# Scoring the cached keys of a decoder step: the products of queries and keys move from GpSimd to VectorE

## The reference, cut to what matters

```
tmat = lax.linalg.triangular_solve(lower + eye, eye, left_side=True, lower=True, unit_diagonal=True)
u = tmat @ (vc * bc[..., None])
w = tmat @ (kb * jnp.exp(gcum)[..., None])
def step(S, xs):
    v_new = u_i - einsum('bhck,bhkv->bhcv', w_i, S)
    o_i = einsum(q_i * exp(g_i), S) + einsum(qk_i, v_new)
    S = S * exp(g_last) + einsum(k_i * exp(g_last - g_i), v_new)
```

```
past_k = cache_k[l][page_table].reshape(Bd, past_len, H_FOX, HEAD_DIM)
s = jnp.einsum('bqhd,bkhd->bhqk', qi, k_all).astype(jnp.float32) * scale
```

## Time and profile before

| | us |
|---|---|
| median of 3 runs | 1795.97 |
| lowest and highest | 1795.91, 1796.79 |
| time of the profiled execution | 1795.97 |
| its span, first to last instruction | 1794.3 |
| what lies around the span | 1.7 |
| the stage `delta_rule`, from 455.6 to 643.3 of the span | 187.7 |
| mean granted TensorE clock of the span | 0.92 |

### The profile page before, as it was taken

How to read it: one execution, slowest core, us unless ns; L and a number is a source line. 1 busy time by engine, 2 the same in 40 slices (tenths; PEclk the granted TensorE clock), 3 DMA queues, 4 the chain that set the end, 5 groups by cost and what they waited for, 6 DMA issues and landing times. The chain is left out here.

```text
span 1794.3 us, 32705 instructions
## 1 busy us (share of the span) xinstructions
PE 1645.4 (92%) x13778; PEld 1513.6 (84%) x13778; DVE 801.2 (45%) x1362; ACT 404.4 (23%) x696; POOL 236.4 (13%) x272
## 2 busy tenths in 40 slices
PE   5999999666899979788799899999999999999995
PEld 5899999564689867465588799999999999999995
DVE  5227862473377622355556333423424424424426
ACT  4210000331222210154555321111111111111112
POOL 3000000240788600011000100000000000000003
PEclk9999999755799975699899899999999999999998
DMA  6011110200223231132243021111110110120122
GB/s 187 24 47 47 47 47 23 90 3 1 72 74 87 61 92 18 53 89 72 101 146 106 26 71 36 48 59 36 48 59 27 55 61 24 49 71 24 47 94 96
DMA packets 113657, 108.52 MB, mean 60 GB/s; under 512 B 16294, under 2 KB 103807, under 8 KB 113509
## 3 DMA queue, kind: packets, MB, share of 16 engines
q1 hardware_dynamic: 110453, 105.56, 19.0%
q0 software_dynamic: 3072, 1.07, 0.5%
HBM read 93.98 MB, written 12.93 MB: 60 GB/s over the span
## 5 line engine op out<-in xcount | busy, mean ns | idle before, releaser
L2354 DVE TENSOR_TENSOR ff_acc<-ff_acc,mf_ps 128x344 f32<-128x344 f32 x264 | 135.3, 513 | 187.4 <-PE mf_ps L2497 187.3
L2490 PE MATMUL mf_ps<-h_lo,ff_w_hi 128*128 128x344 f32 x1008 | 213.8, 320 | 0.0
L2490 PE MATMUL mf_ps<-h_hi,ff_w_hi 128*128 128x344 f32 x1008 | 213.6, 320 | 0.0
L2490 PE MATMUL mf_ps<-h_hi,ff_w_lo 128*128 128x344 f32 x1008 | 212.7, 319 | 0.0
L2497 PE MATMUL mf_ps<-ff_h_hi,ff_d_hi 128*128 128x344 f32 x528 | 170.3, 322 | 3.7 <-DVE ff_h_lo L2349 3.7
L2497 PE MATMUL mf_ps<-ff_h_hi,ff_d_lo 128*128 128x344 f32 x528 | 169.9, 322 | 0.0
L2490 PEld LDWEIGHTS mf_ps<-h_hi,ff_w_lo 128*128 128x128 f32 x1008 | 169.2, 188 | 0.0
L2497 PE MATMUL mf_ps<-ff_h_lo,ff_d_hi 128*128 128x344 f32 x528 | 169.2, 321 | 0.0
L2490 PEld LDWEIGHTS mf_ps<-h_hi,ff_w_hi 128*128 128x128 f32 x1008 | 169.1, 188 | 0.0
L2490 PEld LDWEIGHTS mf_ps<-h_lo,ff_w_hi 128*128 128x128 f32 x1008 | 168.8, 188 | 0.0
L2225 POOL TENSOR_TENSOR ff_x<-ff_x,ff_scaled 128x1024 f32<-128x1024 f32 x7 | 16.4, 2359 | 765.3 <-DVE ff_scaled L2361 765.3
(11 more groups left out here) (424 smaller groups left out, 2637.4 us busy)
## 6 DMA issues: line engine op xcount, KB each, us to landing
fs_keys<-in_cache_k_dram SPq DMA_DIRECT2D x64, 192.0 KB, 2.6
fs_values<-in_cache_v_dram SPq DMA_DIRECT2D x64, 192.0 KB, 2.5
in_raw<-in_w_in_dram SPq DMA_DIRECT2D x22, 512.0 KB, 3.9
ff_raw<-in_w_gate_dram SPq DMA_DIRECT2D x22, 512.0 KB, 3.9
ff_raw<-in_w_up_dram SPq DMA_DIRECT2D x22, 512.0 KB, 4.0
ff_d_raw<-in_w_down_dram SPq DMA_DIRECT2D x22, 512.0 KB, 5.6
ld_x<-in_x_prompt_dram SPq DMA_DIRECT2D x8, 512.0 KB, 6.3
mo_o_raw<-in_w_out_dram SPq DMA_DIRECT2D x8, 512.0 KB, 5.8
```

The costliest lines, as they stand in the source:

```text
L2354: dve.tensor_tensor(part, part, ps[:, b, 0:TG], ALU.add).then_inc(down_added, 1)
L2490: last = pe.matmul(bank(t % 2 * 3 + g)[:, 0:TG], a[:, k], b[:, k, group(g)], start=(k == 0 and n == 0), stop=(k == KD - 1 and n == 2))
```

## The change

The multiplication leaves POOL and is done by DVE, at the head of `score`. `score` of piece r now runs in step r itself and no longer one step later. DVE therefore waits for the query copy and for the loads, which POOL did before; ACT waits for the last score of the sample before and not for its multiplications, before it overwrites `q_rows`. POOL's list loses its 24 multiplications. Nothing else is changed; the same numbers are computed.

```
@@ scalar
-                                act.wait_ge(keys_used, 3 * lo)
+                                act.wait_ge(scored[2], lo)
@@ gpsimd
-                def multiply_keys(b, p):
-                    g0, g1 = PIECES[p]
-                    pool.wait_ge(q_copied, b + 1)
-                    pool.wait_ge(keys_in[p], 16 * (g1 - g0) * (b + 1))
-                    keys = m.fs_keys[:, g0:g1]
-                    pool.tensor_tensor(keys, keys, q_rows[:].unsqueeze(1).broadcast_to([P, g1 - g0, DW]),
-                                       ALU.mult).then_inc(keys_used, 1)
...
-                    if lo is not None:
-                        multiply_keys(lo, r)
@@ vector
                 def score(b, p):
                     g0, g1 = PIECES[p]
+                    dve.wait_ge(q_copied, b + 1)
+                    dve.wait_ge(keys_in[p], 16 * (g1 - g0) * (b + 1))
                     keys = m.fs_keys[:, g0:g1]
+                    dve.tensor_tensor(keys, keys, q_rows[:].unsqueeze(1).broadcast_to([P, g1 - g0, DW]),
+                                      ALU.mult).then_inc(keys_used, 1)
                     dve.wait_ge(keys_used, 3 * b + p + 1)
                     dve.tensor_reduce(m.fs_s[:, b, g0:g1].rearrange("p g h -> p (g h)"),
...
-                    if lo is not None and r > 0:
-                        score(lo, r - 1)
-                    if r == 0 and hi is not None:
-                        score(hi, 2)
+                    if lo is not None:
+                        score(lo, r)
```

## The result

Measured: median 1806.2 us in 5 runs (1804.63 to 1808.16), against 1795.97 in 5 runs of the kernel before on the same chip (1795.88 to 1797.7). The ratio is 1.0055, 95% interval 1.004 to 1.0069: slower by 10.2 us in the medians, where 8.8 were forecast. The profiled execution took 1804.6 us (span 1802.8), so its trace accounts for 8.6 of them; a second profile of the same kernel, taken with the experiments, took 1806.45. Lines up to 1183 keep their place in kernel.py; `score` is now L1261 (multiplication) and L1264 (reduction), and PE's L1388, L1428 and L1458 are L1380, L1420 and L1450.

The account below looks back on a forecast made before the run. PE was taken to bound the middle periods, at 20.03 us each. The terms 10.0 + 1.3 + 1.4 + 0.8 - 4.7 = +8.8 on 1795.97 gave 1804.8 us, with a range of 1794 to 1822 (the forecast's own: 1800 to 1808).

Parts of the forecast that it names:

- The bound: Middle periods: PE is busy for all 20.03 us, so taking 7.1 us off POOL can give nothing there.
- The hold, -4.7: Period 502.17 to 526.93: kept's 6.81 us behind POOL's run ends; the whole excess, 24.76 - 20.03 = 4.7 us, credited.
- The tail, +2.0 a period: DVE from the grams to kd: 2.0 us of added work and 1.2 of POOL contention, partly absorbed; five periods cost 10.0.
- The meetings: DVE instructions with two SBUF inputs waiting for POOL in the tail: 0.7 piece 1, 0.2 kept, 0.3 piece 2; 1.2 us.
- Hidden work in r = 0: Step 0: the score costs DVE 1.75 us more, but the level PE needs moves only to about 9.7, so hidden.
- The first periods, +2.7: First two scored periods: a level PE waits for comes 1.3 us later, then PE's kd wait costs 1.4.
- a clock of 1.00: Sign in the changed profile: PE's granted clock still 1.00, as in the last periods at 11.31 busy of 14.58.
- The last period, +0.8: Last scored period, 604 to 621: DVE is late by 1.4, kept loses 1.17 of contention; kd ends at 622.0 for 621.25.
- B: Step 1's multiplication is held through POOL's run: 1826 if every time, +12 to +15 if once or twice; 0.20 with D.
- D: The 505.94 wait of kept stays or turns up in another period, the rest as summed: 1809.5; 0.20 with B.
- A: DVE's multiplications happen to fall into POOL's gaps, without contention: +1.6, 1797.6 us; chance 0.18.
- C: Faster: added DVE work all hidden, POOL's 4.7 us and 0.5 us of PE's early mask waits go: 1790.8; chance 0.12.

Follow-up runs that it names:

- e8: Changed kernel, piece 2 scored in the next r = 0, piece 1 in r = 1, ACT's query copy later, two POOL waits in r = 2; 1790.96 us.
- e9: Kernel before, DVE multiplying piece 0 alone in r = 0, and POOL waiting once for kept in r = 1; 1790.97 us.
- e1: Kernel before, with one more wait: in r = 1, after its two masks, POOL waits for DVE's kept; 1792.22 us.
- e7: Kernel before, order alone changed: POOL still multiplies, DVE reduces piece r in step r itself; 1796.3 us.
- e3: Changed kernel, POOL made to wait in r = 2 while DVE multiplies pieces 1 and 2 and makes kept; 1793.73 us.
- e5: Changed kernel, with one unused 128x1152 reduction more on DVE (1.34 us) ahead of the score of r = 0; 1806.03 us.
- e2: Kernel before, with DVE multiplying and reducing piece 0 in r = 0, POOL keeping the multiplications of pieces 1 and 2; 1800.54 us.
- e6: Changed kernel, with one unused 128x1152 reduction more on DVE (1.34 us) ahead of the score of r = 1; 1812.55 us.

## Why the prediction was right

*The bound.* Right: PE was full in the middle and POOL's relief gave nothing there. e8 and e9 are back at 20.0 to 20.1 us (one period 20.24) with quite different loads on POOL and DVE, as long as both are in time.

*The hold, -4.7.* Right in cause and size: e1 takes it away alone and gains 4.2 us, and three profiles of the kernel before have it. The change took it away too. The reason given, that POOL's multiplication leaves, was not needed for it: in e7 POOL still multiplies and the hold is gone by the order alone. And the period it stood in did not fall to the length of the others: 23.04 and 23.06 us for 21.54. In both profiles PE comes out of its 1.59 us wait at a lower clock; in the first:

```profile
501.92:524.96 23.04, 21.81 (x583) 20.14 (x583) 17.57 (x26) 5.11 (x11) 12.00 (x11) 0.93 0.26 72
...
501.92 1.55 PE L1420 MATMUL dl_ps<-dl_vb,dl_tt 64*64 64x64 f32 x24 [1.59 <-DVE dl_kd L1328]
503.23 1.52 PE L1422 MATMUL dl_ps<-dl_tt,dl_ke 64*64 64x64 f32 x24
...
506.36 0.91 PE L1380 MATMUL dl_ps<-dl_gcum,head_ones 128*128 128x384 f32 x2
```

From `values_and_keys` to the spread it is 4.44 us, for 2.95 in the middle: the whole 1.5. So 1.5 of the credit of 4.7 was paid back there, which the sum did not have.

*The tail, +2.0 a period.* Measured +1.51. The bare work was put at 0.9, and e3, with the meetings of r = 2 gone, has 20.80 - 20.03 = 0.77. The meetings were put at 1.2 and are 0.55 for piece 1, 0.18 for piece 2 and none for `kept`, 0.73. The multiplications were put at 1.36 and 0.96 and are 1.35 and 0.95. PE waits where it was said: 0.41 for `v_new` (0.7 forecast) and 0.83 for `kd`.

*Hidden work in r = 0.* Right for the changed kernel: e5 adds 1.34 us more there for 0.12. It rests on POOL being out of the way, as e2 shows.

*The first periods, +2.7.* The term that was too small: 2.5 + 2.0 = 4.5 us in the first profile and 3.0 + 3.3 = 6.3 in the second. I had the meetings in it and had named a clock of 1.00 as a sign; it held from the middle on, and not here. From the query spread to the next spread (481.69 to 484.07 before, 480.90 to 484.81 and 482.92 to 487.10 after) PE takes 2.38 us before and 3.91 and 4.18 after without a wait in it, and in the second profile the slow rows go on for 1.4 us more. So the clock is 1.5 and 3.2 us, and what is left, 3.0 and 3.1, is near the 2.7 forecast. The multiplication of piece 2 of the second scored period also meets more of POOL than I had (1.74 us for 0.95).

*The last period, +0.8.* Measured +0.7.

*Sum.* Four tails were 6.0 for 8.0 forecast; the period of the hold was -1.7 for 2.0 - 4.7 = -2.7; the first periods 4.5 or 6.3 for 2.7; the last 0.7 for 0.8. The tails were put too high by 2.0, and the clock, which the sum did not have, cost 3.0 us in the first profile and 4.7 in the second. Errors of opposite sign are why 8.8 stands so near 10.2, and that is luck; the bound, the hold and the places where PE waits were right by the mechanism.

*The rivals.* B, that the multiplication would be held to the end of POOL's run, did not come: of the 24 multiplications none is over 2.02 us. D did not come either: no `kept` is over 0.62. A and C were refuted as forecasts, but e8 and e9 show what C needed: no meeting, and the work out of the tail. What the Trainium skill's page "SBUF — State Buffer" says in its section "Who interferes with whom", that the later one waits until the earlier has finished, fits the rows of the changed kernel shown here, the 1.91 us being one mask's rest; in the kernel before, the measured 6.8 us go against it three times, and so does the `kept` of e1, which waits through two masks.

*Left open.* What decides between a wait of one instruction and the hold of six. In both e1 and the kernel before `kept` asked during the first of POOL's two masks (0.45 us after its start in the earlier trace rows) and was not let in between them. In the changed kernel the multiplication that asks during the first of two masks is let in, and so is another `kept` of the kernel before itself, which asks 0.49 us after the start:

```profile
609.34 2.07 POOL L1183 TENSOR_TENSOR dl_level<-dl_lt,levels 128x384 f32<-128x384 f32 x2
...
609.83 0.72 DVE L1283 TENSOR_TENSOR dl_kept<-state,dl_exps 128x192 f32<-128x192 f32 x1
```

So neither the instruction nor the moment alone tells. Open, too, is why e3's median is 2.5 us below its profiled execution.

## What to carry to other kernels

Work moved between two engines is not priced by their loads but by the point where the receiving engine is next waited for: the same 1.34 us cost 0.12 us a period in one step and 0.79 in the next, nothing and 6 us in the whole. Before moving an instruction with two SBUF inputs to VectorE, look what GpSimd is doing at that moment, and price the other instructions that the move pushes into GpSimd's way. Where one instruction of a group is many times its siblings' length, look at GpSimd's row beside it; a single wait that makes GpSimd stand still there was worth 4.2 us here, with no work moved at all. Where PE has short waits soon after a stretch at half clock, price the slow rows behind them too.

## What the runs showed of the hardware that was not expected

- A VectorE instruction of 0.35 us with both inputs in SBUF took 6.8 us, in the same place in three of three profiles, while GpSimd ran six instructions without a gap; e1 ends it with one wait.
- It works both ways: a pair of GpSimd masks that takes 1.97 us took 3.07 around a VectorE multiplication. Reductions of 1152 elements, with one input, took 1.34 to 1.35 us in every profile, whatever GpSimd did beside them.
- In the first periods, where PE had been at half clock shortly before (0.50 from 457.5 to 469.1 in the second profile of the changed kernel), single waits of 1.6 us were followed by matmuls at a lower clock (0.91 us became 1.65 and 1.23); in the last scored period a wait of 1.76 us was not (the clock stayed 1.00). The place alone does not decide it: in e6 a wait of 1.73 us at 501.30 was followed by rows of the usual length.
